# Carried state of the state-space scan read out for two heads at a time, and the decay rows loaded in another order

## The reference, cut to what matters

```python
cb = einsum("bclgn,bcsgn->bcgls", c_c, b_c)
y_diag = einsum("bcghls,bcsghp->bclghp", cb[:, :, :, None] * decay, xdt)
states = einsum("bclgn,bclgh,bclghp->bcghpn", b_c, decay_to_end, xdt)
chunk_decay = exp(a_cs[:, :, -1])
prev = chunk_state_scan(states, chunk_decay)        # carry * d + s, chunk by chunk
y_off = einsum("bclgn,bcghpn,bclgh->bclghp", c_c, prev, exp(a_cs))
y = y_diag + y_off + x_c * d
y = y * silu(z)                                     # then a norm over each group
```

## Time and profile before

| | |
|---|---|
| runs, median (lowest to highest) | 3979.28 us (3974.26 to 3979.71) |
| profiled execution, its own time | 3975.89 us |
| its span | 3974.2 us |
| mean granted TensorE clock | 0.966 |
| PE, DVE, POOL, ACT busy | 93%, 55%, 29%, 22% |

### The profile page before, as it was taken

The page is one execution under the profiler, slowest core; times in us unless marked ns, Lnnn a source line. Parts: engine busy times, 40 slices in busy tenths (PEclk is TensorE's granted clock), DMA queues, the critical chain, the costliest instruction groups (busy, mean ns, idle before and its releaser), DMA issues.

```text
span 3974.2 us, 44216 instructions
## 1 busy us (share of the span) xinstructions
PE 3697.3 (93%) x17330; PEld 2994.1 (75%) x17330; DVE 2166.8 (55%) x2115; ACT 893.8 (22%) x995; POOL 1141.6 (29%) x505
## 2 busy tenths in 40 slices
PE   7788999999999999998999999979999799989996
PEld 5677878877787887776788888866688688867875
DVE  7698541275843663545421221354289988866534
ACT  3344121121122331211210000112322122224221
POOL 0000433333333222223343443422122121123432
PEclk9989999999999998999999999998999899999998
DMA  3234313351136545533111111113334356664311
GB/s 127 74 80 121 95 42 116 111 169 43 37 127 147 160 137 140 144 93 111 43 47 48 47 48 48 46 23 112 130 120 139 111 158 172 167 209 152 98 51 53
DMA packets 536657, 407.18 MB, mean 102 GB/s; under 512 B 33192, under 2 KB 496424, under 8 KB 536512
## 3 DMA queue, kind: packets, MB, share of 16 engines
q1 hardware_dynamic: 476112, 289.74, 26.7%
q10 hardware_dynamic: 60400, 115.46, 7.8%
HBM read 286.81 MB, written 115.97 MB: 101 GB/s over the span
## 4 chain that ended last, share of the span: by engine, by line
PE 72%; DVE 16%; DVEq 4%; issue 3%; DMA 2%; ACT 2%; POOLq 1%; SPq 0%; POOL 0%; ACTq 0%
PE proj_ps L443 61%; DVE WORK L1112 5%; DVE Hlo L604 1%; DVE AUX L687 1%; PE mix_ps L1295 1%; PE mix_ps L2131 1%; PE mix_ps L2130 1%; ACT stage L471 1%; DVE Hlo L606 1%; PE mix_ps L708 1%; DVEq L685 1%; DVEq L550 1%; PE mix_ps L1442 1%; PE proj_ps L1453 1%; POOLq L413 1%
## 5 line engine op out<-in xcount | busy, mean ns | idle before, releaser
L443 PE MATMUL proj_ps<-Hhi,w_hi 128*128 128x512 f32 x4144 | 1329.1, 402 | 124.3 <-DVE Hlo L604 69.4
L443 PE MATMUL proj_ps<-Hlo,w_hi 128*128 128x512 f32 x4144 | 1289.3, 392 | 0.0
L443 PE MATMUL proj_ps<-Hhi,w_lo 128*128 128x512 f32 x4144 | 1286.7, 392 | 0.0
L411 POOL TENSOR_TENSOR w_hi<-w_raw,zero_col 128x1024 fp32r<-128x1024 f32 (+2 forms) x225 | 424.8, 1888 | 2200.9 <-PE proj_ps L443 1673.4
L443 PEld LDWEIGHTS proj_ps<-Hhi,w_hi 128*128 128x128 f32 x4144 | 772.3, 190 | 326.9 <-issue 89.0
L443 PEld LDWEIGHTS proj_ps<-Hlo,w_hi 128*128 128x128 f32 x4144 | 785.7, 190 | 168.7
L443 PEld LDWEIGHTS proj_ps<-Hhi,w_lo 128*128 128x128 f32 x4144 | 784.1, 189 | 167.5
L414 POOL TENSOR_TENSOR w_lo<-w_raw,w_hi 128x1024 fp32r<-128x1024 f32 (+2 forms) x225 | 579.1, 2574 | 32.0
L1112 DVE SCALAR_TENSOR_TENSOR WORK<-WORK,param_cols 128x1024 f32<-128x1024 f32 x240 | 369.1, 1538 | 18.8
L401 POOL TENSOR_TENSOR w_lo<-w_raw,w_hi 128x1024 fp32r<-128x1024 f32 x48 | 135.4, 2821 | 559.5 <-ACT w_hi L395 559.5
L471 ACT ACTIVATE stage<-proj_ps 128x1024 f32<-128x1024 f32 x104 | 122.0, 1173 | 620.8 <-PE proj_ps L443 619.9
(11 more groups left out here) (419 smaller groups left out, 3603.6 us busy)
## 6 DMA issues: line engine op xcount, KB each, us to landing
w_raw<-in_w_in SPq DMA_DIRECT2D x101, 512.0 KB, 4.5
w_raw<-in_sgu_w_in SPq DMA_DIRECT2D x24, 512.0 KB, 3.9
w_raw<-in_w_out SPq DMA_DIRECT2D x24, 512.0 KB, 4.3
w_raw<-in_w_gate SPq DMA_DIRECT2D x22, 512.0 KB, 3.9
w_raw<-in_w_up SPq DMA_DIRECT2D x22, 512.0 KB, 3.8
w_raw<-in_s_w_in SPq DMA_DIRECT2D x16, 512.0 KB, 4.2
WORK<-mid_acs SPq DMA_DIRECT2D x8, 1024.0 KB, 17.0
mid_qkv<-stage ACTq DMA_DIRECT2D x16, 512.0 KB, 5.2
```

The source lines that it names most:

```text
L411: nc.gpsimd.tensor_tensor(whi[slot][:, 0:kt, :], w, zero_col[:, 0:1].unsqueeze(2).to_broadcast([P, kt, P]), ALU.add)
L443: mm = nc.tensor.matmul(ps[:, h * HALF:(h + 1) * HALF], a[slot][:, k, :], b[:, k, h * HALF:(h + 1) * HALF], start=(k == 0 and n == 0), sto ...
```

## The change

The carried state is read out with 8 matmuls of 128 weight columns, two heads at a time, by the plain C, into `SD_UPD`, and DVE multiplies the result by the exponentials of the decay rows and adds it. For that the decay rows come a second time in another layout: `sd_ea`, 1024 columns, even heads on partitions 0 to 63 and odd heads on 64 to 127, by two DMAs of 256 KB, in two buffers. The buffer of the broadcast rows, `sd_bc`, becomes a single one. ACT takes the exponentials of `sd_ea` and, straight from `sd_bc`, of each head's last value into `sd_cd`, now also two buffers. On SP the decay rows of chunk c+1 are loaded last in chunk c, behind the weight tiles, after the store of chunk c-1 and the exponentials of chunk c; x waits for `mx_y` as well. PE waits for DVE's multiplication (`ssd_carried`) before the state update overwrites `SD_UPD`.

```diff
         def bc_load(sp, c):
-            rows = scratch["acs"][:, c * CH:(c + 1) * CH].unsqueeze(0).to_broadcast([P, SSD_HEADS, CH])
-            sp.dma_start(h16(sd_bc[c % 2]), rows).then_inc(S(f"ssd_bc_in{c % 2}"), 16)
+            rows = scratch["acs"][:, c * CH:(c + 1) * CH]
+            sp.dma_start(h16(sd_bc), rows.unsqueeze(0).to_broadcast([P, SSD_HEADS, CH])).then_inc(S("ssd_bc_in0"), 16)
+            for e in range(2):
+                sp.dma_start(k8(sd_ea[c % 2])[e * SSD_HD:(e + 1) * SSD_HD], rows.rearrange("(k e) c -> e k c", e=2)[e].unsqueeze(0)
+                             .to_broadcast([SSD_HD, KT, CH])).then_inc(S("ssd_bc_in1"), 16)
...
                 if c:
                     sp.wait_ge(S("ssd_ce"), c)
+                    sp.wait_ge(S("mx_y"), c)
                 sp.dma_start(x12, chunk_at("xbc2", c, 0, NXB)).then_inc(S("mx_in"), 16)
                 if c == 0:
-                    bc_load(sp, 1)
                     wait_stored(sp, "z")
                 else:
-                    if c + 1 < NCH:
-                        sp.wait_ge(S("mx_y"), c)
-                        bc_load(sp, c + 1)
                     sp.wait_ge(S("ssd_gated"), c)
                 sp.dma_start(k8(sd_z), chunk_at("z", c)).then_inc(S("mx_side_in"), 16)
                 for m in (2 * c + 2, 2 * c + 3):
                     if m < 16:
                         load_tile(sp, "qkv", m // 2, m % 2)
+                if c + 1 < NCH:
+                    if c:
+                        sp.wait_ge(S("mx_stored"), 16 * c)
+                    sp.wait_ge(S("ssd_ea"), c + 1)
+                    bc_load(sp, c + 1)
...
-                dve.wait_ge(S("ssd_ea"), c + 1)
-                nc.vector.tensor_copy(sd_cd, h16(ea)[:, :, CH - 1])
-                dve.drain()
-                nc.vector.tensor_tensor(g2(ea), g2(ea), x12[:, XBC_C:XBC_C + 2, :].unsqueeze(2).to_broadcast([P, 2, 8, P]), ALU.mult)
                 if c:
                     dve.wait_ge(S("mx_stored"), 16 * c)
...
                 dve.wait_ge(S("mx_y"), c + 1)
+                dve.wait_ge(S("ssd_ea"), c + 1)
+                nc.vector.tensor_tensor(ea, ea, SD_UPD, ALU.mult).then_inc(S("ssd_carried"), 1)
                 nc.vector.tensor_tensor(sd_y, sd_y, PP[0][:, :], ALU.add)
                 dve.drain()
+                nc.vector.tensor_tensor(sd_y, sd_y, ea, ALU.add)
+                dve.drain()
...
                 nc.scalar.activation(sd_s, sd_s, ACT.Exp).then_inc(S("ssd_dec"), 1)
-                nc.scalar.activation(sd_bc[c % 2], sd_bc[c % 2], ACT.Exp).then_inc(S("ssd_ea"), 1)
+                act.wait_ge(S("ssd_bc_in1"), 32 * (c + 1))
+                nc.scalar.activation(sd_ea[c % 2], sd_ea[c % 2], ACT.Exp)
+                nc.scalar.activation(sd_cd[c % 2], h16(sd_bc)[:, :, CH - 1], ACT.Exp).then_inc(S("ssd_ea"), 1)
...
                 for h in range(SSD_HEADS):
                     o = PP[0][(h % 2) * 64:(h % 2) * 64 + 64, (h // 2) * P:(h // 2 + 1) * P]
-                    nc.tensor.matmul(o, sd_xdt[:, h * 64:(h + 1) * 64], h16(sd_s)[:, h, :], start=True, stop=False)
-                    mm = nc.tensor.matmul(o, sd_prev[:, h * 64:(h + 1) * 64], h16(sd_bc[c % 2])[:, h, :], start=False, stop=True)
+                    nc.tensor.matmul(o, sd_xdt[:, h * 64:(h + 1) * 64], h16(sd_s)[:, h, :], start=True, stop=True)
+                for k in range(KT):
+                    mm = nc.tensor.matmul(SD_UPD[:, k * P:(k + 1) * P], sd_prev[:, k * P:(k + 1) * P], x12[:, XBC_C + k // 4, :],
+                                          start=True, stop=True)
                 mm.then_inc(S("mx_y"), 1)
                 b(0)
                 pe.wait_ge(S("ssd_bt"), c + 1)
+                pe.wait_ge(S("ssd_carried"), c + 1)
```

More of the change, by code:

```diff
@@ L1819, in xbc_act @@
                 act.dma_start(scratch["xbc2"][k * P:(k + 1) * P, :], xb[:, k, 4:]).then_inc(S("xbc2_stored"), 16)
[L1822 to L1825, removed]
+        (sd_bc, sd_ea0, sd_ea1, sd_s, sd_x, sd_z, sd_xdt, sd_xdd, sd_y, sd_sq, sd_prev, sd_bt, sd_cb, _, sd_rs, sd_dtr,
+         sd_dt, sd_dta, sd_acs, sd_e, sd_t, sd_u, sd_z2, sd_raw, sd_cd0, sd_cd1, sd_bias, sd_a) = carve(
+            2048, 1024, 1024, 2048, 1536, *[1024] * 6, 256, 256, 48, 256, 1024, *[128] * 8, *[16] * 4)
+        sd_ea, sd_cd = [sd_ea0, sd_ea1], [sd_cd0, sd_cd1]
         h16 = lambda ap: ap.rearrange("p (h c) -> p h c", h=SSD_HEADS)
@@ L1932, in segments @@
                 acs = sd_acs[:, c * SSD_HEADS:(c + 1) * SSD_HEADS].unsqueeze(2).to_broadcast([P, SSD_HEADS, P])
-                dve.wait_ge(S(f"ssd_bc_in{c % 2}"), 16 * (c // 2 + 1))
-                nc.vector.tensor_tensor(h16(sd_s), h16(sd_bc[c % 2]), acs, ALU.subtract)
+                dve.wait_ge(S("ssd_bc_in0"), 16 * (c + 1))
+                nc.vector.tensor_tensor(h16(sd_s), h16(sd_bc), acs, ALU.subtract)
                 dve.drain()
@@ L1939, in ssd_dve @@
                 dt = sd_dt[:, c * SSD_HEADS:(c + 1) * SSD_HEADS].unsqueeze(2).to_broadcast([P, SSD_HEADS, SSD_HD])
-                ea = sd_bc[c % 2]
+                ea = sd_ea[c % 2]
                 dve.wait_ge(S("mx_turned"), c + 1)
@@ L1967, in ssd_dve @@
                     segments(c + 1)
-                nc.vector.tensor_tensor(h16(sd_prev), h16(sd_prev), sd_cd.unsqueeze(2).to_broadcast([P, SSD_HEADS, SSD_HD]), ALU.mult)
+                nc.vector.tensor_tensor(h16(sd_prev), h16(sd_prev), sd_cd[c % 2].unsqueeze(2).to_broadcast([P, SSD_HEADS, SSD_HD]), ALU.mult)
                 dve.drain()
```

## The result

| | before | after |
|---|---|---|
| median of the runs paired with each other | 3979.49 us | 4011.35 us |
| ratio, 95% interval | | 1.0076, 1.0061 to 1.0092 |
| profiled execution, its own time | 3975.89 us | 4006.51 us |
| its span | 3974.2 us | 4004.8 us |
| mean granted TensorE clock | 0.966 | 0.962 |

The account below looks back on a forecast made before the run. PE was taken to bound the kernel. Chunk 2's read-out ending at 1330.5 plus five turns of 32.9 gave 1495.0, +17.9 us: 3975.89 became 3993.8, and 3.4 for the median made 3997 us; range 3984 to 4018.

Parts of the forecast that it names:

- likeliest case: In the scan, a cycle of loads, ACT and store outlasts PE's chunk: +17.9 us, own range 3988 to 4013, chance 0.63.
- E(2): End of chunk 2's read-out on PE: forecast 1330.5, against 1322.7 before.
- The forecast's 2.4 us: Before chunk 0's read-out, less DVE work lets PE begin sooner: about 2.4 us gained, in that chunk only.
- The loop: Per chunk: rows issued, small loads landed, ACT's exponentials, store landed, next rows; 32.9 us against 31.1 for PE's chunk.
- Rows and small loads: On SP's queue: 16.8 us from the rows' issue to their landing, then 7.3 us for the small loads.
- The rate of its own kind: Small loads on SP's queue priced at the 72 GB/s of the existing broadcast: 7.3 us.
- ACT to the store's issue: On ACT: exponentials 0.1 + 1.06 + 0.2, then 1.4 us from L471's start to the store's issue; 2.8 us.
- The store: Store of y, from issue to landing, before the next rows go: 6.0 us taken, 4.5 to 8.4 seen before.
- E(7): End of chunk 7's read-out, by which the scan is judged: forecast 1495.0 against 1477.1 before, +17.9 us.
- rival 2: PE's read-out shrinks 1.8 us a chunk through cheaper full-width passes and parallel halves: -17 us, 3962 us, chance 0.08.
- Rival 1: Small loads on SP's queue take only 1.6 us: +5 to +9, so 3986 us, chance 0.14.
- Rival 3: PE's idle 1.8 us a chunk drops its clock, PE losing 3.4 us each chunk: +37, 4016 us, chance 0.15.

## Why the prediction was right, and where it was off

**Side and range.** Slower had 0.75 of the chance, and 4011.35 us lies in the range, beyond the 3997 of the forecast but within the likeliest case's own range.

**The start of the scan.** E(2) was to be 1330.5 and is 1330.4. That it hits so closely is luck: chunk 1's rows were issued at 1248.7 instead of 1252.9, their small loads then needed 27.2 us instead of 25.6, chunk 0's store 7.2 instead of 6.0, and x came 4.5 us behind chunk 2's small loads instead of 2.4; the misses cancel. Chunk 0 gave nothing, as said: from the first rows to E(0) it took 43.6 us against 42.5. Without the small loads chunk 0 does give: from the first rows to E(0) 36.6 us, against 42.5 before. The forecast's 2.4 us took only DVE's work; the rest fits the half-clock stretch behind the old wait, since the granted clock was 1.00 from 1223 to 1260 there.

**The loop.** It is there, with the links named. The step that failed is its sum, 32.9 us a turn; the five chunks behind E(2) averaged (1505.4 - 1330.4) / 5 = 35.0. The terms, as averages over the five turns from 1285.7 to 1460.5:
- *Rows and small loads*: 16.8 + 7.3 = 24.1 forecast, 15.2 + 9.8 = 25.0 measured. The rows are quicker, the small ones slower. "The rate of its own kind" did not carry over: the small loads land 8.9 to 10.3 us behind the rows. Nearly doubling them cost 13.2 us a chunk.
- *ACT to the store's issue*: 2.8 forecast, 2.9 measured (2.5 in three turns; in the first ACT was not free when they landed, 4.2).
- *The store*: 6.0 forecast, on the ground that no rows are in flight then. Measured 7.0, between 6.0 and 8.2: x, held back behind the small loads, and with it z and a weight tile, run just when the store does.
- Two us a turn over five turns are 10 us, which is E(7)'s miss, 1505.4 against 1495.0.

**What the loop is worth.** The prediction put the whole loss on the loop through the store. The run without the store's wait shows a second one, through the weight tile, the loads and x, of 32.7 us a chunk at its shortest. The forecast had x landing 2.4 us behind the small loads (2.6 to 4.5 measured) and did not follow that on as a limit of its own. Only taking the loads away ends both.

**The read-out.** Forecast 3.9 us against 3.7 before. By the measure of that 3.7, up to the start of the next L443, it is 1359.75 to 1363.45, again 3.7; up to DVE's start it is 1359.75 to 1363.73, 4.0, against 3.8 before. So it did not shrink, and the forecast 0.2 us a chunk is at most that: with the exponentials moved a chunk lasted 30.8 us, against 30.9 before the change. The 32 half-width passes take 1.90 us, 0.059 each, with the halves changing at every matmul; the 16 full-width ones 1.8 up to the start of the next, 0.11 each. The Trainium skill, "TensorEngine Tiling (Array Packing)", Key Properties, lets tiles work in parallel; nothing of that shows here in either kernel, so rival 2 fell with both its halves. The squares began at E + 5.0 and PE wanted them at E + 7.1: hidden, as said.

**Rival 1**, quick small loads, fell: 9 to 10 us, not 1.6.

**Rival 3**, the clock, came in part. Three windows of the kernel after, one chunk each:

```profile
1330.40:1363.70 33.30, 30.97 (x179) 25.38 (x178) 19.69 (x15) 9.51 (x10) 8.48 (x5) 1.00 0.71 166
1363.70:1400.10 36.40, 32.58 (x179) 26.72 (x179) 19.68 (x15) 9.51 (x10) 8.48 (x5) 0.95 0.71 153
1400.10:1437.70 37.60, 33.59 (x180) 27.72 (x179) 19.69 (x15) 9.51 (x10) 8.54 (x5) 0.91 0.63 149
```

The work is the same, but PE is busy 1.6 and 2.6 us longer where the granted clock averages 0.95 and 0.91, behind waits of 3.8 and 4.0 us for x. It averaged 0.95 in chunks 1 and 6 too, behind waits of 3.4 and 2.6 us. "1.8 us is less than half of that idle time" was right of the forecast's idle time, and chunks 2 and 3, where PE waited about 2 us, kept the full clock. The loop's longer turns let PE wait longer. How much of the loss is the clock's is not settled, but it can be little: the turns between the issues of rows are accounted for by loads, ACT and store, in which ACT waited for PE 0.7 and 0.3 us in two turns (L471), and the last read-out, at the full clock, ends 16.7 us behind x's landing at 1488.7, as forecast.

## What to carry to other kernels

A load that is added to a queue must be priced by its kind (a broadcast here ran at less than a quarter of an ordinary load's rate) and together with everything behind it in that queue, since its first victim is the next load's reader. Having found one loop longer than the bounding engine's stage, look for the others that share its slowest link: taking out a wait ended one loop here and shortened the scan by 6 of its 28 us, taking out the link won them all. Before a long broadcast is moved, ask which store on another queue it will then overlap, and who waits for that store to reuse its buffer.

## What the runs showed of the hardware

**Broadcasts to 64 partitions are slower than to 128.** Two windows of the kernel after, the first while the rows to 128 partitions are on their way, the second while the small ones are:

```profile
1354.00:1369.00 15.00, 15.00 (x95) 11.94 (x94) 6.43 (x7) 1.30 (x2) 4.26 (x2) 1.00 0.63 77
1369.00:1372.00 3.00, 3.00 (x20) 2.67 (x19) 2.92 (x2) 2.06 (x2) 0.00 (x0) 1.00 0.53 37
```

77 GB/s against 37. By the landings 512 KB of them took 8.9 to 10.3 us behind the rows, 51 to 59 GB/s, the last of it with x already moving. Why was not tried.

**A store on another queue is held up by a broadcast.** It is issued by ACT, the broadcast by SP, and it lands 4.2 us after its issue with none in flight (no small loads), and, by the medians, after 7.9, 11.1 and 23.2 us in the three kernels that issue the rows shortly before it. In the last of the three, the kernel with the rows ahead of the tile, it lands within 0.2 us of the last small load (1387.89 and 1387.92). A window of this kernel, in which the store has been issued too:

```profile
1363.00:1372.00 9.00, 9.00 (x43) 7.47 (x42) 6.23 (x4) 0.38 (x1) 3.18 (x2) 1.00 0.33 76
```

76 GB/s at a DMA share of 0.33: no more than the rows had alone, with two thirds of the engines' time unused. The packets of each queue (count, MB, share) tell more; q1 is SP's, q10 is ACT's. First 1362 to 1375, while the rows are on their way, where ACT's queue moved nothing (its first packets follow in the next microsecond, 2 us before the rows land):

```profile
q1 hardware_dynamic: 1868, 0.96, 39.7%
```

then 1379 to 1383, beside the small loads:

```profile
q1 hardware_dynamic: 297, 0.15, 28.3%
q10 hardware_dynamic: 299, 0.15, 12.6%
```

The Trainium skill, "DMA: Bandwidth & Descriptors", Queues, rings and completion order, has each DMA engine take packets from its queues in turn, by which a store of 512 KB would share with the broadcast. Beside the small loads the trace agrees, with 299 packets against 297; beside the rows it does not, with none against 1868 although two stores of ACT's had been issued at 1362.9 and 1363.3. The measurement decides; what holds the stores back there stays open.
